# Differential attention in a fused inference step: the second softmax row combined on three engines instead of one

## The reference

```
def diff_attention(q, k, v, lam):          # per head two sets of queries and keys, a = 0, 1
    def one_block(qblk):                   # 128 queries
        s = jnp.einsum('bqhad,bkhad->bhaqk', qblk, k).astype(F32) * scale
        p = jax.nn.softmax(s, axis=-1)
        a = p[:, :, 0] - lam * p[:, :, 1]
        return jnp.einsum('bhqk,bkhv->bqhv', a.astype(v.dtype), v)
```

## Time and profile before

| | |
|---|---|
| median of 3 runs | 2843.72 us |
| the profiled execution, its own time | 2845.1 us |
| its span, first to last instruction | 2843.3 us |
| TensorE products, busy | 2721.0 us (96%) |
| VectorE busy | 1798.9 us (63%) |
| ScalarE busy | 884.6 us (31%) |
| GpSimd busy | 871.4 us (31%) |
| mean granted TensorE clock | 0.987 |

### The profile page before, as it was taken

One profiled execution on the slowest core, in us unless ns is written; L12 is line 12 of the kernel. 1 busy time (PEld: TensorE's weight loads), 2 busy tenths in 40 slices (PEclk: granted clock), 3 DMA queues, 4 the chain that ended last, 5 costly groups with the idle time before them and its releaser, 6 DMA issues. The chain is left out here.

```text
span 2843.3 us, 41885 instructions
## 1 busy us (share of the span) xinstructions
PE 2721.0 (96%) x16344; PEld 2595.5 (91%) x16344; DVE 1798.9 (63%) x2662; ACT 884.6 (31%) x1454; POOL 871.4 (31%) x392
## 2 busy tenths in 40 slices
PE   7998888999999999999999998899999999999998
PEld 5997777999999999999899997559999999999997
DVE  6798986755666666666658614545466666666665
ACT  4213666251122222221542231542512222222214
POOL 0673123422222222222412121434322222222223
PEclk9999999999999999999999999999999999999999
DMA  6543101500111111110335434323101111111102
GB/s 251 182 149 97 18 21 42 204 30 31 45 44 44 44 44 44 44 44 30 124 116 185 169 122 178 130 82 139 45 30 45 44 44 44 44 44 44 44 30 82
DMA packets 64072, 227.29 MB, mean 80 GB/s; under 512 B 8080, under 2 KB 18768, under 8 KB 58576
## 3 DMA queue, kind: packets, MB, share of 16 engines
q1 hardware_dynamic: 62368, 225.12, 22.8%
q10 hardware_dynamic: 1584, 0.51, 0.1%
HBM read 191.52 MB, written 29.88 MB: 78 GB/s over the span
## 5 line engine op out<-in xcount | busy, mean ns | idle before, releaser
L1538 DVE SCALAR_TENSOR_TENSOR x<-ps,mod,x 128x384 f32<-128x384 f32 (+2 forms) x944 | 493.6, 541 | 397.2 <-PE ps L222 397.2
L220 PE MATMUL ps<-hh,wi_hi 128*128 128x384 f32 x2112 | 708.6, 336 | 8.2 <-ACT hid L1132 4.5
L222 PE MATMUL ps<-hh,wi_lo 128*128 128x384 f32 x2112 | 706.2, 334 | 0.0
L221 PE MATMUL ps<-hl,wi_hi 128*128 128x384 f32 x2112 | 706.1, 334 | 0.0
L1294 POOL TENSOR_TENSOR wi_lo<-raw_in,wi_hi 128x1024 fp32r<-128x1024 f32 x80 | 197.7, 2471 | 1016.8 <-ACT wi_hi L1113 1016.8
L220 PEld LDWEIGHTS ps<-hh,wi_hi 128*128 128x128 f32 x2112 | 396.9, 188 | 10.9 <-ACT hid L1132 5.2
L221 PEld LDWEIGHTS ps<-hl,wi_hi 128*128 128x128 f32 x2112 | 397.1, 188 | 0.8
L222 PEld LDWEIGHTS ps<-hh,wi_lo 128*128 128x128 f32 x2112 | 396.9, 188 | 0.0
L220 PE MATMUL ps<-fac_hi,wo_hi 128*128 128x384 f32 x656 | 221.0, 337 | 4.0 <-DVE x L1538 3.2
L1113 ACT ACTIVATE wi_hi<-raw_in 128x1024 fp32r<-128x1024 f32 x80 | 84.7, 1059 | 444.2 <-PE ps L222 444.2
L222 PE MATMUL ps<-fac_hi,wo_lo 128*128 128x384 f32 x656 | 219.9, 335 | 0.0
(11 more groups left out here) (325 smaller groups left out, 5679.6 us busy)
## 6 DMA issues: line engine op xcount, KB each, us to landing
raw_in<-in_w_ffn_in_dram SPq DMA_DIRECT2D x80, 512.0 KB, 3.6
wmt<-in_w_mod_t_dram SPq DMA_DIRECT2D x56, 512.0 KB, 3.6
wo_raw<-in_w_ffn_out_dram SPq DMA_DIRECT2D x22, 1024.0 KB, 4.8
gla_spill<-turn SPq DMA_DIRECT2D x22, 576.0 KB, 3.7
oraw<-in_w_in_odd_dram SPq DMA_DIRECT2D x24, 512.0 KB, 5.2
wmt_odd<-in_w_mod_t_dram SPq DMA_DIRECT2D x24, 512.0 KB, 4.3
x<-in_x_dram SPq DMA_DIRECT2D x8, 1152.0 KB, 9.9
wm<-in_w_mod_dram SPq DMA_DIRECT2D x16, 512.0 KB, 11.8
```

What stands on the lines that cost most here:

```text
L220: pe.matmul(acc, w_hi, in_hi, start=first, stop=False, skip_group_check=resumed)
L221: pe.matmul(acc, w_hi, in_lo, start=False, stop=False, skip_group_check=resumed)
L222: return pe.matmul(acc, w_lo, in_hi, start=False, stop=last, skip_group_check=resumed)
L1538: last = dve.scalar_tensor_tensor(out=x[:, ft, cols], in0=ps[:, bank, loc], scalar=mod[:, layer, GATE2 * KT + ft, v:v + 1], in1=x[:, ft, c ...
```

## The change

Of the 1152 columns of a unit's combination, VectorE does the first 512 (`SPLIT`), as before in one instruction. The other 640 are multiplied by w1 on ScalarE, in place in p1, and added to p0 by GpSimd. w1 itself becomes a product with two per-row scalars (`tensor_scalar`), with no second tensor input. TensorE's transposes of blocks 4 to 7 wait for GpSimd's sum; those of blocks 0 to 3 for VectorE's part. The block u0 (128 columns) stays on VectorE whole. GpSimd's other work is placed at certain units, each behind the addition of that unit. Side products change places: `output` goes from u4-u6 to u5-u7, three `mix` from u7 to u4.

```
-            mix_units = [(0, u) for u in range(4, 9)] + [(1, 7), (1, 8), (2, 7), (2, 8), (3, 1), (3, 2), (3, 3)]
+            mix_units = [(0, u) for u in range(4, 9)] + [(1, 4), (1, 8), (2, 4), (2, 8), (3, 1), (3, 2), (3, 3)]
...
-                        side[h * UN + 4 + r] = ("output", h - 1, r)
+                        side[h * UN + 5 + r] = ("output", h - 1, r)
...
-                def combine(n):
+                def weigh(n):
                     h, u, r = n // UN, n % UN, n % 2
-                    w = CTX if u == 0 else T
                     dve.wait_ge(exped, 2 * n + 2)
                     dve.reciprocal(rs1[:, r:r + 1], esum[:, h % 2, 1, u:u + 1]).then_inc(weighed, 1)
                     dve.wait_ge(weighed, 2 * n + 1)
-                    dve.scalar_tensor_tensor(out=w1[:, r:r + 1], in0=rs1[:, r:r + 1], scalar=esum[:, h % 2, 0, u:u + 1],
-                                             in1=neglam[:], op0=ALU.mult, op1=ALU.mult).then_inc(weighed, 1)
+                    if n >= 3:
+                        dve.wait_ge(combined_rest, n - 2 - (n - 2) // UN)
+                    dve.tensor_scalar(w1[:, r:r + 1], rs1[:, r:r + 1], esum[:, h % 2, 0, u:u + 1], neglam[:],
+                                      ALU.mult, ALU.mult).then_inc(weighed, 1)
                     dve.wait_ge(weighed, 2 * n + 2)
+                    w = CTX if u == 0 else SPLIT
                     dve.scalar_tensor_tensor(out=prob[0][r][:, 0:w], in0=prob[1][r][:, 0:w], scalar=w1[:, r:r + 1],
                                              in1=prob[0][r][:, 0:w], op0=ALU.mult, op1=ALU.add).then_inc(combined, 1)
...
+                def weigh_rest(n):
+                    r = n % 2
+                    if n % UN:
+                        act.wait_ge(weighed, 2 * n + 2)
+                        act.activation(prob[1][r][:, SPLIT:T], prob[1][r][:, SPLIT:T], ACT.Copy,
+                                       scale=w1[:, r:r + 1]).then_inc(weighed_rest, 1)
...
                     if 2 <= n < UNITS + 2:
                         out_of_psum(n - 2)
+                    if 1 <= n <= UNITS:
+                        weigh_rest(n - 1)
                     if n >= 3:
                         square(n - 3)
...
+                def combine_rest(n):
+
+                    r, done = n % 2, n - 1 - n // UN
+                    if n % UN == 0:
+                        return
+                    pool.wait_ge(combined, n + 1)
+                    pool.wait_ge(weighed_rest, done + 1)
+                    pool.tensor_tensor(prob[0][r][:, SPLIT:T], prob[0][r][:, SPLIT:T], prob[1][r][:, SPLIT:T],
+                                       ALU.add).then_inc(combined_rest, 1)
...
-                for h in range(HEADS):
-                    if h >= 1:
-                        scales(h - 1)
-                        normalise(h - 1)
-                    if h + 1 < HEADS:
+                for n in range(1, UNITS + 1):
+                    h, u = n // UN, n % UN
+                    combine_rest(n - 1)
+                    if h >= 1 and h < HEADS:
+                        if u == 3:
+                            scales(h - 1, range(3))
+                        elif u == 4:
+                            scales(h - 1, range(3, 5))
+                            normalise(h - 1)
+                    if h == HEADS - 1 and 5 <= u:
+                        mixed_low(u - 5)
+                    if h + 1 < HEADS and u == 5:
                         q_low(h + 1)
+                    if h + 1 < HEADS and u == 8:
                         k_low(h + 1)
-                    else:
-                        for g in range(HEADS):
-                            mixed_low(g)
-                    if h >= 1:
-                        output_low(h - 1)
+                    if h >= 2 and u == 0:
+                        output_low(h - 2)
                 weights.split(pool, 0)
...
                     if r == 0:
                         pe.wait_ge(combined, n + 1)
+                    elif r == 1:
+                        pe.wait_ge(combined_rest, n - n // UN)
```

More of the change, by code:

```diff
@@ L1737, in attention @@
             weighed, combined = sem("weighed"), sem("combined")
+            weighed_rest, combined_rest = sem("weighed_rest"), sem("combined_rest")
+            SPLIT = 4 * P
             turned, at_out = sem("turned"), sem("at_out")
@@ L1877, in _ @@
                     if 1 <= n <= UNITS:
-                        combine(n - 1)
+                        weigh(n - 1)
                     if n < UNITS:
@@ L1986, in k_low, with scales @@
                                        ALU.subtract).then_inc(qk_low, 1)
-                def scales(h):
+                def scales(h, steps):
                     r, n = h % 2, 5 * h
[L1990 to L2000, removed]
+                    for step in steps:
+                        if step == 0:
+                            pool.wait_ge(squared, UN * (h + 1))
+                            pool.wait_ge(inverted, h + 1)
+                            pool.tensor_tensor(oscale[:, r], ss[:, r], rinv[:, r], ALU.mult).then_inc(final_step, 1)
+                            continue
+                        pool.wait_ge(final_step, n + step)
+                        if step == 2:
+                            pool.tensor_scalar(oscale[:, r], oscale[:, r], 1.0 / P, EPS, ALU.mult, ALU.add).then_inc(final_step, 1)
+                        elif step == 3:
+                            pool.tensor_tensor(oscale[:, r], oscale[:, r], half[:], ALU.pow).then_inc(final_step, 1)
+                        else:
+                            pool.tensor_tensor(oscale[:, r], oscale[:, r], rinv[:, r], ALU.mult).then_inc(final_step, 1)
                 def normalise(h):
```

## The result

| | kernel before | changed kernel |
|---|---|---|
| median | 2844.38 us (6 runs, 2843.61 to 2848.04) | 2860.82 us (6 runs, 2858.89 to 2862.69) |
| the profiled execution, its own time | 2845.1 | 2859.31 |
| its span | 2843.3 | 2857.5 |

The ratio is 1.0054, 95% interval 1.0041 to 1.0067: slower by 16.4 us. Forecast were 2854.0 and a range of 2841 to 2862. Between the profiled executions the difference is 14.2 us, and 14.8 had arisen by the end of the attention stage: the first split of an output weight (`even_out_wlo`) behind the barrier starts 14.83 us later than before, and from there on the shift stays between 12.5 and 16.4.

The account below looks back on a forecast made before the run. The bound was the loop scores, first maximum, two exponentials, scores, with VectorE late in few units. Heads 0 to 2 at +3.0, +3.0, +3.4, head 3's terms and plain units' +0.5 total +10.3 us: 2843.7 becomes 2854.0, range 2841 to 2862.

Parts of the forecast that it names:

- the lower clock: TensorE's slow scores in head 3's u5 go, 7.71 to 7.16, -0.55 us; each slow block elsewhere costs 1.2.
- (d): At u0 of heads 2 and 3, o_lo on GpSimd holds the short combination; maxima 0.45 us late, twice.
- ScalarE's idle time: Units with a high-part cast have none, so the copy's 0.70 us makes u4 7.01 and u7 7.20.
- (a): k_lo in u8 follows the addition; the next head's first scores wait: 7.95 instead of 6.51, +1.44 us, three times.
- (b): q_lo, moved from u4 to u5, holds the rotary product; maxima 1.14 us late (head 0), 0.51 (heads 1, 2).
- (c): In u4 of heads 1 to 3, power and normalisation on GpSimd hold the combination; maxima of u5 0.7 us late.
- plain units: Units with little beside them: the scaled copy fits ScalarE's 0.57 us idle, costing 0.1 each, five times, +0.5.
- (e): p_lo in head 3 ends before or near the moment the combination wants the port: nothing lost.
- head sums: New minus old unit lengths added up by head: +3.0 us in head 0, +3.0 in head 1, +3.4 in head 2.
- The first rival: VectorE is the bound and gets faster: 5.5 us and the slow scores' 1.2 come back, 2837; chance 0.15.
- The second: No collision with GpSimd's port: (b), (c), (d) gone, 5.2 us less, 2848.8; chance 0.13.
- The third: Scaled copy costs 1.15 us, lengthening units and starting GpSimd's work 0.35 later: 8 more, 2862; chance 0.12.

Follow-up runs that it names:

- experiments 4 and 6: 4: changed kernel, VectorE combining all 1152 columns, 0.9981. 6: copy early, all scales steps at u3, normalisation alone at u4, 0.9984; same placement without split, 0.9983.
- experiment 1: Changed kernel with ScalarE's scaled copy moved ahead of the ninth block's copy: 2844.97 us, 0.9991 of the kernel before.
- the run with filler: Changed kernel with TensorE's side work in u2 of heads 1 to 3 written again during its pause: 2856.22 us, 1.0038 of the kernel before.
- the last kernel: Changed kernel with copy early, all scales steps at u3, normalisation alone at u4, and repeated side work in u2 of heads 1 to 3: 2843.09 us, 0.9985.

## Why the prediction came out as it did

The mechanism and nearly all unit lengths were right, the side of the result too. One term was much too small, that of the lower clock, booked at -0.55 us in one unit, and one, (d), too large.

| step | forecast | measured in the changed kernel |
|---|---|---|
| copy, addition, combination | 0.80, 1.55, 0.75 | 0.82, 1.54, 0.75 where unhindered |
| ScalarE's idle time: u4, u7 | 7.01, 7.20 | 6.96, 7.11 to 7.14; back to 6.5 with the copy early |
| (a) k_lo: u8 | 7.95 | 7.88 or 7.89, three times |
| (b) q_lo holds the rotary product: u6 | head 0 +1.14, heads 1, 2 6.97 | head 0 +0.97, 6.94 and 6.96 |
| (c) normalisation: u5 of heads 1 to 3 | 7.16 | 7.18, 7.17, 7.16; 6.46 with it placed late |
| (d) o_lo: maxima of u1, heads 2, 3 | 0.45 late | 0.10 and 0.08 late; u1 +0.07, +0.05 |
| plain units | 5 x 0.1 | u0 of heads 1 to 3 +0.17 (head 1 in the second profile) |
| (e) p_lo and the weight, head 3: u4 | 7.01 | 6.92 |
| head sums 0, 1, 2 | +3.0, +3.0, +3.4 | +3.03, +5.37, +3.83 |
| head 3 up to its u8, and from there on | -0.7, +1.1 | +1.32, +1.48 |

In (d) the collision came as forecast, but hardly cost anything. Head 2, the end of u0 and the start of u1:

```profile
377.68 2.67 POOL L2024 TENSOR_TENSOR o_lo<-qkvu,o_hi 128x1152 fp32r<-128x1152 f32 x1
...
377.76 2.73 DVE L1835 SCALAR_TENSOR_TENSOR prob<-prob,w,prob 128x128 f32<-128x128 f32 x1
...
380.42 2.61 DVE L1843 TENSOR_REDUCE nmax<-ps 128x1 f32<-128x1152 f32 x2
```

The short combination took 2.73 us instead of 0.35. It ended with o_lo, and the maxima began at once, at S+2.00 of u1, 0.10 late; I had added another 0.3 behind o_lo, and u0 itself had become 0.16 longer, which moved the scores away. (e) had p_lo collide with nothing; it held two combinations of head 3 to 1.57 us. One of them is in the last unit, and behind it the end of the stage came out 0.4 above the forecast; that this is the cause was not tested.

Two readings of rows were loose. From the exponentials to the next scores it takes 2.65 us behind k_hi, but 2.80 behind q_hi (336.79 to 339.59). And the maximum that I took from rows 5, at 342.38, had no GpSimd instruction beside it; the pair at 335.02, which overlaps q_lo, took the same 2.62 us for two, so the conclusion stands.

The first rival, VectorE as the bound, is refuted by experiments 4 and 6: without the split and with it the units are alike but for 0.5 us in u2. The second, no collision with GpSimd's port, is refuted by the 2.21, 2.45 and 1.57 above. The third, a longer chain, is refuted by the copy's 0.82, though its time of 2862 was the nearest of all: a reminder that a total close to a rival's says little while its parts can be looked at. The two places where the port's rule carried the forecast stand: the Trainium skill, "SBUF — State Buffer", section "SBUF: two separate sides", has GpSimd and a VectorE instruction with two SBUF inputs shut each other out, and these traces agree: 2.21 instead of 0.75 on VectorE, and 3.14 instead of 2.11 on GpSimd in experiment 1.

The mis-sized term is TensorE's clock. I wrote that some blocks of slow scores may come or go, and booked only one that goes (in head 3's u5, 0.55 in the sum). It went, and three came. Against the run with filler, the changed kernel lost 1.19 and 1.30 in head 1 (u0, u3), 0.86 and 1.54 in head 2 (u2, u3), 0.87 and 1.56 in head 3 (u2, u3), 7.3 us in all; the kernel before had lost 0.27 and 1.26 in head 2. Taken out of both, heads 1 to 3 up to u8 of head 3 come to +2.9, +3.0 and -1.1 us, where I had +3.0, +3.4 and -0.7; the 0.4 that are left in heads 2 and 3 are (d). The price that I gave for a slow block, 1.2 us, fits most of them, but where the transposes ahead of the scores ran slow too, in heads 2 and 3, one stretch cost 2.4. What failed was to treat them as noise of zero mean. In heads 1 to 3 of the trace before, both slow blocks stood behind a pause of TensorE, of 3.23 and 2.78 us, and two more pauses, of 3.23 and 2.49, passed without one. The moved placement kept such a pause in u2 of heads 1 to 3 (2.78, 2.78 and 2.49 us), and I had the numbers to ask whether it would be struck there. How often it is struck could not be read from them: in the changed kernel it was in all three heads in both profiles, with the filler in none, and the two stretches of u0 and u8 in head 1 had no such pause. The Trainium skill, "TensorE: Matmul & The Clock Gate", section "HAM oscillation — how this bites in real kernels", describes products throttled again and again because each group waits for its data. The two profiles of the changed kernel agree, with 0.60 of the clock behind a pause of 2.78 us, and the kernel before, with a pause of 3.24 us and a full clock behind it, shows that not every such pause is struck.

Two expectations of mine on experiments missed as well, for the same reason: the weight alone (3.4 us gained, 4.0 lost to the clock) and the last kernel (a stage 3.6 us shorter than without the filler, no shorter time). The total was 6.8 us low. The head sums, the 1.48 behind them and a start that was 0.20 earlier make the 14.83 at the end of the stage, 4.5 above my 10.3; the parts behind gave back 0.6. That the shift arrived nearly whole, as I had assumed, is luck: in three other profiles those parts moved it by 4.3 to 5.7 us. The medians lie 2.2 further apart than the profiled executions; and the kernel before has 0.7 more in its median of six runs than in that of three.

## What to carry to other kernels

Before work is moved off the busiest engine, find out whether that work lies on the path from one step to the next; here it lay under the scores in all but a few units, and giving it to two other engines mostly lengthened their queues. When a chain of three engines is added inside a step, the place of its middle link in that engine's queue can be worth as much as its whole length: moved 1.5 us earlier, the same copy turned 16 us of loss into none, as did cutting it to one column. Count TensorE's pauses before and after an edit, and give the clock a term of its own in the sum. Judge a stage by its own length in the trace beside the total time: here a kernel gained 5 us in time with a stage 1 us longer.

## What was not expected of the hardware

- A one-column product with one tensor input and two per-row scalars ran its 0.27 us in the middle of a 2.64 us GpSimd subtraction; the same product with a second tensor input had taken 2.52. What differs is the number of tensor inputs, as the Trainium skill, "SBUF — State Buffer", section "Who interferes with whom", has it; the trace agrees, for a size of one column too. Put into the kernel before, it brought head 3's u4 from 8.63 to 6.45.
- A pause of TensorE of 2.78 us with nothing in it was followed by transposes and scores at 0.60 of the clock; with 1.31 us of repeated products in it, by a full clock. Yet 3.24 us of pause passed without harm in one kernel and 1.92 did not in another, and three slow stretches had no pause over 1.29 us in their own unit or the one before it.
- The parts behind the stage, which no edit touched, took from 4.3 us less to 5.7 us more than in the kernel before, in different kernels' profiled executions and with no order by when the stage ended.
- A VectorE combination of 128 columns, 0.35 us alone, took 2.73 beside a GpSimd subtraction of 2.67 that had started 0.08 us ahead.
